# A transformer and expert kernel: its adaLN start, its router and the loading of its first expert blocks rearranged

## The reference

```python
mod_x = (jax.nn.silu(c) @ w_ada[l] + b_ada[l])[:, None, :]
sh_a, sc_a, g_a, sh_m, sc_m, g_m = jnp.split(mod_x, N_MOD, axis=-1)
hx = _modulate(_rmsnorm(x, norm_attn[l]), sh_a, sc_a)      # h * (1 + scale) + shift; the same for ctx with c_ctx
qa, ka, va, qb, kb, vb, ga, gb = proj(hx)
x = x + g_a * _merge(ya, yb, ga, gb, w_oa[l], w_ob[l], w_out[l])
hx = _modulate(_rmsnorm(x, norm_mlp[l]), sh_m, sc_m)
x = x + g_m * moe(hx.reshape(b * s, d)).reshape(b, s, d)
```

## Time and profile before

| | us |
|---|---|
| median of 3 runs | 1844.12 (1842.15 to 1846.11) |
| profiled execution | 1841.82 |
| its span, first to last instruction | 1839.5 |
| TensorE busy | 1687.6 (92%) |
| VectorE, ScalarE busy | 547.6 (30%), 266.2 (14%) |
| moved from HBM | 535.17 MB, 292 GB/s over the span |
| granted TensorE clock, mean | 0.986 |

### The profile page before, as it was taken

The page is one execution under the profiler, slowest core; times in us unless marked ns, Lnnn a source line. Parts: engine busy times, 40 slices in busy tenths (PEclk is TensorE's granted clock), DMA queues, the critical chain, the costliest instruction groups (busy, mean ns, idle before and its releaser), DMA issues.

```text
span 1839.5 us, 18325 instructions
## 1 busy us (share of the span) xinstructions
PE 1687.6 (92%) x7206; PEld 892.6 (49%) x7206; DVE 547.6 (30%) x1065; ACT 266.2 (14%) x552; POOL 29.2 (2%) x30
## 2 busy tenths in 40 slices
PE   4999999899989899898898988977999999989998
PEld 1544676534333233232332423323777788678743
DVE  2342432333323223233242232323022221210355
ACT  2123441301000010000000000001143222010000
POOL 0110000000000000000000000001000000000000
PEclk9999999899999999999999999999999999999999
DMA  9867225399999999999999999999532334244320
GB/s 369 296 239 220 75 104 203 126 419 428 431 429 430 430 428 430 430 430 431 428 430 430 429 430 429 430 429 406 189 128 95 135 112 149 107 147 173 138 92 23
DMA packets 86887, 536.99 MB, mean 292 GB/s; under 512 B 4624, under 2 KB 5776, under 8 KB 62256
## 3 DMA queue, kind: packets, MB, share of 16 engines
q1 hardware_dynamic: 84736, 530.60, 71.1%
q10 hardware_dynamic: 2096, 5.64, 0.9%
HBM read 535.17 MB, written 1.05 MB: 292 GB/s over the span
## 4 chain that ended last, share of the span: by engine, by line
PE 70%; DMA 26%; DVE 1%; ACT 1%; issue 1%; SPq 1%; DVEq 0%; POOL 0%; POOLq 0%; ACTq 0%
PE ps L1466 33%; PE ps L1731 19%; DMA ring<-in_w_up 11%; DMA ring<-in_w_gate 10%; PE ps L2049 5%; PE ps L1719 3%; PE ps L1782 2%; DMA arena<-in_w_down 2%; DMA arena<-in_w_up 2%; DMA ring<-in_w_ada 1%; PE ps L1479 1%; PE ps L1620 1%; SPq L372 0%; PE ps L1572 0%; PE ps L1595 0%
## 5 line engine op out<-in xcount | busy, mean ns | idle before, releaser
L1731 PE MATMUL ps<-ring,arena 128*64 128x512 f32 x2304 | 512.1, 595 | 57.2 <-DMA ring<-in_w_gate 28.7
L1466 PE MATMUL ps<-arena,ring 128*128 128x256 f32 x1856 | 412.7, 382 | 3.0 <-ACT arena L723 2.7
L1466 PEld LDWEIGHTS ps<-arena,ring 128*128 128x128 f32 x1856 | 353.1, 191 | 62.2 <-issue 7.1
L1731 PEld LDWEIGHTS ps<-ring,arena 128*64 128x64 f32 x2304 | 164.1, 137 | 386.2 <-issue 317.1
L1466 PE MATMUL ps<-ring,arena 128*128 128x512 f32 (+1 forms) x480 | 197.1, 566 | 4.6 <-issue 3.4
L1731 PE MATMUL ps<-arena 128*64 128x512 f32 x768 | 174.8, 604 | 13.4 <-DMA arena<-in_w_up 11.1
L1466 PEld LDWEIGHTS ps<-ring,arena 128*128 128x128 f32 x480 | 89.7, 190 | 103.6 <-issue 99.6
L680 ACT ACTIVATE arena<-ps 128x512 f32<-128x512 f32 x32 | 19.1, 597 | 676.7 <-PE ps L1753 676.7
L1731 PEld LDWEIGHTS ps<-arena 128*64 128x64 f32 x768 | 53.4, 139 | 127.9 <-issue 108.2
L1782 PE MATMUL ps<-arena 128*128 128x512 f32 x128 | 68.8, 666 | 21.1 <-DVE xres L1168 19.6
L1133 DVE TENSOR_TENSOR arena<-ps,arena 128x512 f32<-128x512 f32 x32 | 22.1, 691 | 210.7 <-PE ps L1731 210.7
(11 more groups left out here) (252 smaller groups left out, 1029.4 us busy)
## 6 DMA issues: line engine op xcount, KB each, us to landing
ring<-in_w_up SPq DMA_DIRECT2D x56, 2048.0 KB, 33.8
ring<-in_w_down SPq DMA_DIRECT2D x56, 2048.0 KB, 30.7
ring<-in_w_gate SPq DMA_DIRECT2D x48, 2048.0 KB, 34.5
ring<-in_w_in SPq DMA_DIRECT2D x23, 2048.0 KB, 8.3
arena<-in_w_gate SPq DMA_DIRECT2D x16, 2048.0 KB, 29.3
arena<-in_w_up SPq DMA_DIRECT2D x16, 2048.0 KB, 28.3
arena<-in_w_down SPq DMA_DIRECT2D x16, 2048.0 KB, 35.3
ring<-in_w_ada SPq DMA_DIRECT2D x12, 2048.0 KB, 15.0
```

The costliest lines, as they stand in the source:

```text
L1466: last = pe.matmul(dst, a, b, start=k == 0, stop=k == len(terms) - 1)
L1731: mm = pe.matmul(dst[CAP * g:CAP * g + CAP, :], stationary(half, c), w[:, c, 512 * g:512 * g + 512], start=half == 0 and c == 0, stop=half ...
```

## The change

- The first four adaLN blocks are now row blocks: 256 rows by all 2048 columns (pieces of 8 KB), accumulated over the four in one bank (`ada_first`). One copy, one turn and one addition take the place of four each. The tiles are transposed between these products and copied to `hT` unmodulated; scale and shift are applied in place afterwards, and the projections s = 0 and s = 2 wait for each feature chunk by itself.
- The kB block is loaded right behind kA and vA ("keys first"); the adaLN products 4 to 7 stand at s = 8 to 11, not 4, 6, 8, 10.
- ACT issues the constants in three parts, and the rows and gate biases behind the first copy.
- The router takes the residual transposed without normalising and with the scale alone; the inverse root multiplies the logits, and the shift's share of them is one product with permuted weights (`rwp`, loaded by eight small DMAs during attention). The shift is added to the gathered tokens instead.
- DVE makes mask, ranks and S4 first, weights and the number of passes behind them. PE waits for the latter only after the first pass over the experts.
- The fourth gather round stands between the halves of the first gate.
- A ninth block, the second half of the first up matrix, has a place of its own in the arena (`ASIDE`). Its load waits for the last output product.
- The down bias is added in the last group.

```diff
-W_ADA1, W_KVA, W_KB, W_QA, W_QB, W_VB = 0, 4, 7, 9, 11, 15
-W_ADA2 = (5, 6, 8, 10, 12, 13, 14, 16)
+W_ADA1, W_KVA, W_KB, W_QA, W_QB, W_VB = 0, 4, 5, 8, 11, 15
...
-            return {4: 4, 6: 5, 8: 6, 10: 7, 12: 8, 13: 9, 14: 10}.get(s)
+            return {8: 4, 9: 5, 10: 6, 11: 7, 12: 8, 13: 9, 14: 10}.get(s)
...
         def ada_bank(n):
-            return n % 2 if n < 4 else 6
+            return 6 if n else 0
         def mod_bank(n):
-            return 2 + n % 2 if n < 4 else 7 if n < 11 else 5
+            return 2 if n == 0 else 7 if n < 11 else 5
...
             for i in range(4):
-                load_cols(W_ADA1 + i, t["w_ada"], 512 * i)
+                load(W_ADA1 + i, ada1_view(i), t["w_ada"][2 * P * i:2 * P * i + 2 * P, 0:2 * D]
...
+            def first_loads(X, u, first):
+                for k in (0, 1, 2):
+                    free = W_MOE - RING + k + 1 if first else u * GROUP_BLOCKS + (X["before"] - MRING + k + 2)
+                    sp_.wait_ge(X["used"], free)
+                    block_load(X, 0, 0, k // 2, k % 2, k)
+                for k, (q, m) in ((4, (1, 0)), (6, (1, 1)), (8, (0, 2)), (10, (2, 0))):
+                    for half in range(2):
+                        n = k + half
+                        if n == 5 and first:
+                            sp_.wait_ge(sem("merged_done"), 4)
+                        if n == 4 and first:
+                            sp_.wait_ge(X["used"], W_MOE - RING + 4)
+                        elif n in (7, 8) and first:
+                            sp_.wait_ge(X["used"], W_MOE - RING + n - 2)
+                        elif n > 8 and first:
+                            sp_.wait_ge(X["used"], X["before"] - MRING + n)
+                        elif not first:
+                            sp_.wait_ge(X["used"], u * GROUP_BLOCKS + (X["before"] - MRING + n + 1))
+                        block_load(X, 0, q, m, half, n)
+                        if n == 8:
+                            if first:
+                                sp_.wait_ge(sem("wo_done"), 4)
+                            block_load(X, 0, 0, 1, 1, ASIDE)
...
+                first_loads(X, u0, first)
+                group_loads(X, u0, 0, False, 4)
...
-            act.dma_start(const[:, :], t["const"]).then_inc(sem("const_in"), 16)
-            act.dma_start(row[:, :], t["row"].broadcast_to([P, N_ROW])).then_inc(sem("small_in"), 16)
-            act.dma_start(g_attn[:, :], t["b_ada"][:, 2 * D:3 * D].broadcast_to([P, D])).then_inc(sem("small_in"), 16)
-            act.dma_start(g_moe[:, :], t["b_ada"][:, 5 * D:6 * D].broadcast_to([P, D])).then_inc(sem("small_in"), 16)
-            act.dma_start(wf_t[:, :], t["w_forget"]).then_inc(sem("small_in"), 16)
...
+            turned(3)
+            act.dma_start(const[:, C_ROPEC:N_CONST], t["const"][:, C_ROPEC:N_CONST]).then_inc(sem("row_in"), 16)
+            act.dma_start(row[:, :], t["row"].broadcast_to([P, N_ROW])).then_inc(sem("row_in"), 16)
...
+            modulation(0)
+            act.dma_start(const[:, P:C_ROPEC], t["const"][:, P:C_ROPEC]).then_inc(sem("const_in"), 16)
+            act.dma_start(g_attn[:, :], t["b_ada"][:, 2 * D:3 * D].broadcast_to([P, D])).then_inc(sem("small_in"), 16)
+            act.dma_start(g_moe[:, :], t["b_ada"][:, 5 * D:6 * D].broadcast_to([P, D])).then_inc(sem("small_in"), 16)
+            act.dma_start(wf_t[:, :], t["w_forget"]).then_inc(sem("small_in"), 16)
+            act.dma_start(bshift.rearrange("p (h c) -> p h c", h=2),
+                          t["b_ada"][0:1, 3 * D:4 * D].rearrange("o (h d c) -> d (o h) c", h=2, c=4)).then_inc(sem("small_in"), 16)
             act.wait_ge(sem("mod_ready"), 1)
-            for j in range(0, KC, 2):
-                act.wait_ge(sem("ht_tr"), j + 1)
-                for m in range(2):
-                    last = act.activation(hT[:, j, T * m:T * m + T], bank(4 + j % 4)[:, T * m:T * m + T],
-                                          ACT.Identity, scale=scale_a[:, j, m:m + 1], bias=modT[:, j, m:m + 1])
-                last.then_inc(sem("ht_act"), 1)
+            for m in range(2):
+                for j in range(4):
+                    a = hT[:, j, T * m:T * m + T]
+                    act.activation(a, a, ACT.Identity, scale=scale_a[:, j, m:m + 1],
+                                   bias=modT[:, j, m:m + 1]).then_inc(sem("ht_act"), 1)
...
             for i in range(4):
+                if i % 2 == 0:
+                    act.wait_ge(sem("root_done"), 17 + i // 2 + 1)
                 act.wait_ge(sem("hp_tr"), i + 1)
                 act.activation(hperm[:, i // 2, i % 2].rearrange("p c d -> p d c"),
-                               bank(4 + i).rearrange("p (d c) -> p d c", c=4), ACT.Copy).then_inc(sem("hp_read"), 1)
+                               bank(4 + i).rearrange("p (d c) -> p d c", c=4), ACT.Copy,
+                               scale=rstd[:, i // 2:i // 2 + 1]).then_inc(sem("hp_read"), 1)
...
+                    for j in (2 * r, 2 * r + 1):
+                        last = act.activation(xeT[:, j, :], bank(4 + r % 2)[:, T * (j % 2):T * (j % 2) + T],
+                                              ACT.Identity, bias=modT[:, 24 + j, 0:1])
...
+            def best(i):
+                dve.wait_ge(sem("logit_done"), i + 1)
+                dve.scalar_tensor_tensor(logit[:, i, 0:N_EXP], bank(2 * i)[:, 0:N_EXP], rstd[:, i:i + 1], crow,
+                                         ALU.mult, ALU.add)
+                dve.drain()
+                dve.max(top8[:, i, :], logit[:, i, 0:N_EXP])
+                dve.drain()
...
+                dve.match_replace(out=lrep[:, i, :], in_to_replace=top8[:, i, :], in_values=logit[:, i, :],
+                                  imm_value=BIG)
+            dve.wait_ge(sem("wo_done"), 1)
+            dve.tensor_tensor(crow, bank(3)[:, 0:N_EXP], row[:, R_RB:R_RB + N_EXP], ALU.add)
             x1_add(0, 0)
             x1_add(0, 1)
-            norm_tile(xn2, 0, "ssm_done", "hm_xn")
-            x1_add(1, 0)
-            hm_out(0)
-            x1_add(1, 1)
-            norm_tile(xn2, 1, "ssm_done", "hm_xn")
-            hm_out(1)
...
+            mean_tile(0)
+            x1_add(1, 0)
+            hm_out(0, 4, 8, bank(5), 2)
+            root()
+            x1_add(1, 1)
+            mean_tile(1)
+            hm_out(1, 6, 8, bank(3), 5)
+            best(0)
+            root()
+            best(1)
             dve.drain()
             dve.tensor_scalar(emask, lrep[:, :, 0:N_EXP], BIG, None, ALU.is_equal).then_inc(sem("mask_done"), 1)
...
+            xn_transpose(0)
+            ada_first(0)
+            xn_transpose(1)
+            ada_first(1)
+            xn_transpose(2)
+            ada_first(2)
+            xn_transpose(3)
+            ada_first(3)
+            mod_transpose(0)
...
-                last = product(dst[:, 0:cols], [(hT[:, j, P * tile:P * tile + P], w[:, j, :]) for j in range(KC)])
+                order = [j // 2 + 4 * (j % 2) for j in range(KC)]
+                if s in (0, 2):
+                    for n, j in enumerate(order):
+                        modulated(tile // 2, j)
...
+            pe.wait_ge(sem("rw_in"), 144)
+            pe.wait_ge(sem("modm_ready"), 1)
+            product(bank(3)[:, 0:N_EXP], [(modT[:, 24 + j, 0:1].broadcast_to([P, P]), rwp[:, j, :]) for j in range(KC)])
...
             out_product(mergedT, W_OUT, 1, 1, "wo_done")
...
+            pe.wait_ge(sem("x1_done"), 3)
+            turn(1, 0, 4, bank(6))
+            pe.wait_ge(sem("hm_act"), 1)
+            pe.wait_ge(sem("hm_dve"), 1)
+            pe.wait_ge(sem("const_in"), 16)
+            product(bank(0)[:, 0:N_EXP], [(hmT[:, j, 0:P], rw[:, j, :]) for j in range(KC)]).then_inc(sem("logit_done"), 1)
+            pe.wait_ge(sem("x1_done"), 4)
+            turn(1, 4, 6, bank(7))
+            turn(1, 6, 8, bank(3))
+            for j in range(KC):
+                if j == 0:
+                    pe.wait_ge(sem("hm_act"), 2)
+                if j == 4:
+                    pe.wait_ge(sem("hm_act"), 3)
+                if j == 6:
+                    pe.wait_ge(sem("hm_dve"), 2)
+                last = pe.matmul(bank(2)[:, 0:N_EXP], hmT[:, j, P:T], rw[:, j, :], start=j == 0, stop=j == KC - 1)
+            last.then_inc(sem("logit_done"), 1)
...
             pe.wait_ge(sem("mask_done"), 1)
-            ones, strict = cst(C_ONES), cst(C_STRICT)
-            product(bank(1)[:, 0:N_EXP], [(strict, emask[:, 0, :])])
-            product(bank(1)[:, N_EXP:2 * N_EXP], [(ones, emask[:, 0, :]), (strict, emask[:, 1, :])])
-            product(bank(1)[:, 2 * N_EXP:3 * N_EXP], [(ones, emask[:, 0, :]), (ones, emask[:, 1, :])]
+            pe.matmul(bank(1)[:, 0:TT * N_EXP], strict, emask.rearrange("p t e -> p (t e)"), start=True, stop=False)
+            pe.matmul(bank(1)[:, N_EXP:TT * N_EXP], ones, emask[:, 0, :], start=False, stop=True).then_inc(sem("rank_done"), 1)
+            turn_back(1, 0)
+            turn_back(1, 1)
```

(16 more changed lines are left out.)

519 lines of the change are left out of this document (285 added, 234 removed).

## The result

| | before | changed |
|---|---|---|
| median of 4 runs each | 1845.11 us | 1815.51 us |
| lowest to highest | 1842.15 to 1847.79 | 1813.42 to 1817.92 |
| ratio (95% interval) | | 0.984 (0.9823 to 0.9858) |
| the profiled execution | 1841.82 | 1817.92 |
| its span | 1839.5 | 1816.1 |

Predicted were 1821.0 us and the range 1814 to 1829. The changed kernel is faster by 29.6 us by the medians, and by 23.4 us of span between the two profiled executions: that of the kernel before was shorter than all of its four runs, that of the changed kernel is the longest of its four. One execution of the changed kernel in a later series (after_again) took 1983.7 us at a mean granted clock of 0.846, where the others have 0.985 to 0.990; it is in no ratio and no comparison here.

A forecast was written before the change was run, and what follows sets the result against it. The expert stage was taken as bound by its weight loads, so time saved earlier carries to the end. 8.4 - 0.7 + 15.4 = 23.1 us off 1841.8 gave 1818.7, plus 2.3 for the median 1821.0; range 1814 to 1829.

The forecast's parts named there:

- The start: From kernel begin to first projection: effective start moves from 45.7 to 37.3 us, a gain of 8.4, between 4.9 and 11.9.
- Fourth block: Start: fourth adaLN block lands at 29.2 instead of 35.7 us, 5.5 from fewer bytes ahead and 1.0 from longer runs.
- The last adaLN product: Start: takes 2.8 us, between 1.92 at the high clock and 3.62 at the low, ending at 32.0.
- The five DMA issues: Start, on ACT behind the copy to the arena: 2.4 us with a small gap, in front of the modulating copies.
- The low clock of the first projection: Start: up to 3.3 us lost if the first projection begins at the low clock; 1.7 taken.
- Attention and merge: Between start and router: 0.5 us lost to eight small DMAs, 0.2 to one more router product; loss 0.7.
- The router: Last output product to first expert load: 13.0 us earlier at the high clock, 10.5 at the low; 11.75 taken.
- The ninth block: Start of the expert load stream: block 12 lands 23.7 us after the first issue, before 27.35; gain 3.65, between 2.5 and 4.9.
- my own case: Whole kernel: median within 3 us of 1821; chance 0.54.
- Low clock in both stages: Rival for start and router: last adaLN product, projection and gather lose 3.8 us in all, giving 1824.8; chance 0.17.
- High clock in both: Rival for start and router: both run at the high clock, giving 1817.2 us; chance 0.10.
- rival 5: Weight ring loses its lead: PE waits 7.4 us for each of eight blocks, 36 us slower net, 1880; chance 0.03.

The follow-up runs named there:

- after_again: The changed kernel run once more, unchanged; median 1815.5 us, ratio 0.9844 to the kernel before.
- old_start: Changed kernel with its start undone: adaLN column blocks, constants ahead, one root, modulation as the turned tiles leave PSUM; median 1824.93 us.
- tables_first: Changed kernel with the weight table and number of passes made ahead of the selection, the first gather behind them; median 1825.74 us.
- no_ninth: Changed kernel with the ring of eight expert blocks and the old order of first loads; median 1819.85 us.
- consts_first: Changed kernel with the seven deferred DMAs (about 2.1 MB) issued behind the context tiles as before; median 1824.01 us.
- gather_four: Changed kernel with the fourth gather round back ahead of the first gate product; median 1815.20 us.
- normalised_turn: Changed kernel with each router tile normalised ahead of its turn, as before; median 1820.92 us.
- values_order: Changed kernel with the keys' weights back at place 7 of the stream and adaLN products from the fifth projection on; median 1822.11 us.
- fill_two: Changed kernel plus unread 256-column products at the start (1 and 4), ahead of the last combination (3) and the pass-count branch (5); median 1815.88 us.
- early_count: Changed kernel plus unread products at the start, fourth gather round before the gate, ScalarE copies before DMA issues, pass count read behind first up product; 1812.41 us.

## Why the prediction was right, and where it was not

**The path.** Right: the expert stage runs at its loads, so a microsecond off start or router is one at the end. old_start, tables_first and no_ninth each show a part carried whole (8.3, 8.4 and 4.7 us at the landing, 9.4, 10.2 and 4.3 by the medians).

**The start**, 8.4 forecast, near 9.9 measured. Fourth block landed near 29 (its product starts at 29.06): the sum of 5.5 for bytes and 1.0 for runs holds, its split doesn't. With the bytes back (consts_first) that product starts 3.2 us later and not 5.5, and 4.8 come together only at the next block. So more than 1.0 came from the longer runs or the new order of work; the rate is 434 GB/s in 24 to 26 us (before 387), but no run separates the two. The last adaLN product was put at 2.8, half low clock; it took 1.92, at 2.4 GHz. The tile turns stand right ahead of it, but old_start, without them and behind a wait of 1.20 us, took 1.92 too, so that they are the cause isn't shown. The five DMA issues were put behind the copy; the timeline shows the first of them issued with it, at 31.05, so ScalarE's copies start 0.5 us behind the scale (32.86 to 33.37), and the chain from product to projection is 3.1 us, not 3.6. The low clock of the first projection was put at 1.7, and is 5.30 - 3.62 = 1.7. **The keys-first order** I had as a place that costs nothing; that it has to stand there for the rest to arrive, 4.5 us, I had not said.

**Attention and merge**, a loss of 0.7 forecast, none found: from first projection to first output product 256.7 us before; now 258.0, less the 1.7 of the projection's clock, 256.3. The added router product took the place of the 1.68 us wait there. Start and merge together were 7.7 forecast and 10.2 measured; this is the sum that was mis-sized most.

**The router**, 11.75 forecast, 12.8 measured by the first load, 12.9 by the up product. Mask 6.3 (6.8 forecast), gather 9.2 (9.2), first load 18.8 (18.6 at the high clock). The forecast had 2.45 us between the levels and took the middle; the clock did fall to 0.50 at 328, but came back in the first round, and at 0.77 to 1.00 the 24 products took 5.96 us, as they do in gather_four (7.97 for 32). By the experiments, up to the first load: order of tables and selection 8.7, turning ahead of normalising 5.4, gate inside the gather 2.5. That is 16.6, more than the whole, so the parts overlap and can't be added. Up to the up product the third is -0.7, but there the whole also holds the down bias, 3.69 us of products that stood between gate and up before; no run put it back. The forecast took the low clock of the gather in the kernel before for the effect of the wait right ahead of it. The trace has it falling earlier, ahead of that wait, in a window that TensorE was busy for all of:

```profile
339.00:341.00 2.00, 2.00 (x14) 2.00 (x14) 0.68 (x6) 0.40 (x1) 0.00 (x0) 0.63 0.00 0
```

Two shorter waits, of 1.81 and 1.51 us, lay before that window, so what brought the clock down there stays open.

**The ninth block**, 3.65 forecast, 3.4 between the two traces, 4.2 by no_ninth. The mechanism was partly wrong: I counted holes from the first freed block, but gather_four issues that load 2.4 us later and lands 0.7 us earlier.

**The sum** at the last landing: 23.1 forecast, 26.4 measured, of which the profiled execution lost 3.0 in the tail. The forecast of the profile was 1818.7 and it came at 1817.9, nearer than its parts deserve: two errors of 3 us that cancel, which is luck. The tail's 3.0 are differences of clock. The turns took 3.68 for 1.97 us and the first group of products 16.07 for 14.05; but the kernel before had its own dip in the next group, 15.75 us for 14.06, so that both make 1.9 net. The other 1.1 lie near the end, where the 512 records of products from 1598.4 us on take 113.6 us (before 112.5): the granted clock in 1601 to 1605 is 0.61, at the same place before (1626 to 1630) 0.96.

```profile
1252.00:1256.00 4.00, 2.27 (x11) 2.27 (x12) 1.62 (x4) 1.30 (x6) 2.40 (x3) 0.57 1.05 387
```

Of the kernel before:

```profile
1300.92 15.75 PE L1466 MATMUL ps<-arena,ring 128*128 128x256 f32 x64
```

The other traced executions have tails of 582 to 586 us where no fill stands there, so nothing shows that the change lengthens it. The medians differ by 29.6 us, the landings by 26.4; the remaining 3 us are within what runs differ by, and which share of them is chance stays open.

**The number.** The median, 1815.5, lies in the range but 5.5 us below 1821.0, outside the 3 us of my own case. Only 0.8 of the 5.5 is the profiled execution (1817.9 for 1818.7). The rest is the step from profile to median: I added 2.3 us, because the profiled execution before lay that far below its median, and the changed kernel's lay 2.4 above.

**The rivals.** Low clock in both stages, by the section "The HAM clock gate" of the page "TensorE: Matmul & The Clock Gate" of the Trainium skill: the traces agree in the first projection of six traces and in the router of normalised_turn (0.70 in 322 to 324, where TensorE had been busy for 0.43 of the 2 us before). They don't in the last adaLN product (1.00), and not in the router of gather_four, tables_first and consts_first, where the clock fell with no wait ahead of it. High clock in both (1817.2) was nearest in number and wrong in the projection. The ring kept its lead: TensorE is busy for 113.8 of 115 us in 50 to 165. Slower, rival 5, didn't come true, though values_order and consts_first show the first blocks of the ring arriving late (2.68 and 3.37 us) once order or bytes are put back.

## What to carry to other kernels

Ask of every stage that you make faster what it will reach sooner. Here the new start would have run into its fifth block, and an order of loads that was worth nothing before was worth 4.5 us after. In a stage bound by its loads, find what the stream's phase follows (here the last landing stood 884 us behind the first up product, wherever the first block came free) before you pull a single free block forward. And put work that nobody waits for behind the selection that TensorE does wait for: a wait of 5.55 us on TensorE cost 8.7, since a clock that had already fallen stayed low through it.

## What the runs showed that I had not expected

- The clock can fall while TensorE is busy. In gather_four's router, with no wait of note before it, the windows read:

```profile
322.00:324.00 2.00, 2.00 (x20) 2.00 (x19) 0.78 (x5) 1.89 (x5) 0.36 (x1) 1.00 0.91 238
324.00:326.00 2.00, 2.00 (x15) 2.00 (x15) 1.33 (x10) 0.10 (x1) 0.20 (x1) 0.76 1.00 426
326.00:328.00 2.00, 1.85 (x10) 1.45 (x9) 0.88 (x7) 1.95 (x2) 0.00 (x0) 0.50 1.05 379
328.00:330.00 2.00, 2.00 (x12) 2.00 (x10) 1.82 (x5) 1.13 (x2) 0.00 (x0) 0.50 0.98 346
```

  Ahead of it were router products of 32 columns and turns, PEld as busy as PE. The router falls to 0.50 in every trace but old_start's, which has 1.00 throughout. Three gather rounds took 5.4 to 8.5 us, by where the low stretch lay; how much of the difference between runs this makes, and what in those products lets the clock fall, no run shows.
- Ahead of the branch on the pass count TensorE issues nothing for 2.9 to 3.5 us, and products placed in front don't hide it (fill_two); with the count read earlier the stretch ends with VectorE's tile at 2.6 (early_count). The reading is thus some 0.8 us of it or more; what the rest is wasn't tried.
- A wait for a small DMA can hold the first work of a kernel: the sigmoid waits for a 128-column piece of the constants to 13.41 us, 7.6 us behind its table. It doesn't read that piece; the change made the two share a count. Where it waits for its own tensor alone it ran at 7.20 (before) and 8.08 (old_start). Whether the wait costs anything at the end no run shows, since none takes away this wait alone.
